# Stick-breaking attention: the sums over keys from a rounded high half and a low half of the summand

## The chip, the core and the metric

The kernel runs on one core of a Trainium2 chip. The metric is the device time of one execution in microseconds (us). Before the change it is 1397.66 us, the median of three runs (1396.64 to 1399.08). The engines are TensorE (PE; its weight loads are listed as PEld), VectorE (DVE), ScalarE (ACT), GpSimd (POOL) and SyncE (SP), which issues the weight transfers.

## What is computed

A decoder trunk of two layers on x of 256 tokens x 1024 features in float32, batch 1: layer 0 is sliding-window attention (16 heads of 64, window 128, sinks) and a dense SwiGLU of 2816; layer 1 is stick-breaking attention (16 heads of 64) and a mixture of 8 experts of 3584 with two chosen for each token; then a final RMSNorm. The change is in the second attention, which the reference gives as:

```
z = einsum(q, k) * scale                                  # query t, key s
log_fail = where(before, log_sigmoid(-z), 0.0)            # before: s < t
between = lax.cumsum(log_fail, axis=3, reverse=True) - log_fail
a = where(before, exp(log_sigmoid(z) + between), 0.0)
out = einsum(a, v) @ w_o
```

The kernel keeps z with keys on the 128 partitions and queries along the free dimension. With softplus(z) = -log_sigmoid(-z), the exponent of a is z minus the sum of softplus over the keys from s up to the query. That is a sum over partitions, so TensorE makes it as a product with a triangular matrix of -1 (and, from the second key block to the first, with a full matrix of -1), added to the z that stands in PSUM.

## The kernel before

Every weight product runs on rounded numbers (the type float32r). A weight unit of 1 MB (128 partitions x 4 x 512) comes by DMA into one of 7 raw slots; ScalarE makes its rounded high half (L528), VectorE its low half, raw minus high (L533), up to three units ahead of TensorE; TensorE adds three products for each pair (high x high, high x low, low x high). A raw slot is loaded again when its low half is done. The inputs of the products (inT_high, inT_low, and hid_high, hid_low in the dense layer and the experts) are split in the same way. All matmuls are recorded on L1354, the transposes on L1406, L1515, L1700 and L1731.

Each engine has its own list of instructions, written out by hand, that it runs in order; semaphores tie the lists together. The eight PSUM banks are given out by a table (`plan`), and the scores of tile b take two banks, (2b) mod 6 and the next.

The second attention goes by feature tiles n = 0 to 7, each with two heads (`half`). For a tile:

- `sb_scores(n)` on TensorE: z = k q in float32 into two banks, 384 columns each: for the first key block 256 queries, for the second the last 128. Then a product of mask_scale with mask_tri (both rounded), which puts -1e30 on what is not before the query. It signals z_ready.
- `clamp(b)` on VectorE (L1164): soft = min(z, 30), 128 x 768, from both banks.
- `log_one_plus_exp(b)` on ScalarE (L851, L853): exponential, then logarithm of 1 + it.
- `soft_plus(b)` on VectorE (L1172): fail = max(z, soft), the summand, float32 in SBUF. It signals fail_ready.
- `sb_sums(n)` on TensorE: three float32 products for each half, with tri or minus_ones as the other operand, onto the z in the banks.
- ScalarE's exponential of the banks (L866) gives stick, the weights a.
- `sb_values(n)` on TensorE: v times stick in float32.

The tiles soft, fail and stick have two buffers each, all in the area `work` (so the profile shows them as work; q is in qT, k and v in kv_area, tri in consts). Scores and clamp of tiles 0 and 1 come before the projection of v, and their maxima during it. Then TensorE runs `sums(n)`, `scores(n+2)`, `values(n-1)` for n = 0 to 8, as far as there are such tiles. VectorE runs, for b = 2 to 7, `clamp(b)`, at b = 5 and 7 the low half of a finished part of the attention's output (L1020), and `soft_plus(b)`. ScalarE runs `stick(c)`, at odd c from 3 on the rounded half of a part of the output (L750), and `log_one_plus_exp(c+2)`. GpSimd has nothing between 57 and 419 us. After the loop comes the output projection wo1, whose first product reads weight units and output parts that are ready by then.

Of the kernel before, what the change touches and what calls it, by code (L numbers as in the profile page):

```python
# [14 lines left out]
P = 128  # L15
# [281 lines left out]
def build(nc, a):  # L297

    ctx = ExitStack()
    with ctx:  # L300
        def sb(name, shape, dt=F32):
            return ctx.enter_context(nc.sbuf_tensor(name, shape, dt))

        def sem(name):
            return ctx.enter_context(nc.semaphore(name))
# [17 lines left out]
        minus_ones = sb("minus_ones", [P, P])  # L323
        bias_tiles = sb("bias_tiles", [QKV_TILES, P])
# [6 lines left out]
        vT_swa = sb("vT_swa", [P, SEQ])  # L331
# [49 lines left out]
        probs = work[:, 2 * w0:3 * w0]  # L381

# [7 lines left out]
        fail = [work[:, (2 + n) * 768:(3 + n) * 768].rearrange("p (a k) -> p a k", a=2) for n in range(2)]  # L390
        stick = [work[:, (4 + n) * 768:(5 + n) * 768].rearrange("p (a k) -> p a k", a=2) for n in range(2)]
# [61 lines left out]
        fail_ready = sem("fail_ready")  # L453
        stick_used = sem("stick_used")
# [188 lines left out]
        def _(pool):  # L643
# [12 lines left out]
            for n in range(2):  # L656
                for m in range(2):
# [14 lines left out]
                                    router_gain[:, :].unsqueeze(2).to_broadcast([P, DT, E]), ALU.mult).then_inc(router_ready, 1)  # L672

# [272 lines left out]
        def _(dve):  # L946
# [5 lines left out]
            def split_to(n):  # L952

                while lows[0] <= n:
                    make_low(dve, lows[0])
                    lows[0] += 1
# [163 lines left out]
            V.tensor_copy(mask_tri[:, :], tri).then_inc(masks_ready, 1)  # L1120
            split_to(AT["wo0"] + SPLIT)
# [39 lines left out]
            def clamp(b):  # L1161
                lo = 2 * b % 6
                dve.wait_ge(z_ready, b + 1)
                V.tensor_scalar(soft[b % 2], bank[:, lo:lo + 2, 0:3 * P], SOFT_TOP, None, ALU.min).then_inc(clamped_ready, 1)  # L1164

            def soft_plus(b):
                lo = 2 * b % 6
                dve.wait_ge(soft_ready, b + 1)
                if b >= 2:
                    for half in range(2):  # L1170
                        full(dve, ("z", b - 2, half))
                V.tensor_tensor(fail[b % 2], bank[:, lo:lo + 2, 0:3 * P], soft[b % 2], ALU.max).then_inc(fail_ready, 1)  # L1172

            clamp(0)
# [3 lines left out]
            soft_plus(1)  # L1178
            for vh in range(2):
                split_to(AT["v1"] + vh + 1 + SPLIT)  # L1180
                for tb in range(TB):
                    b = full(dve, ("v1", vh, tb))
                    freed(V.tensor_copy(v_sb[:, tb, vh * HALF:(vh + 1) * HALF], b), ("v1", vh, tb))
            for b in range(2, FT):
                clamp(b)
                if b >= 5 and b % 2 == 1:
                    input_part_low("oT1", b // 2 - 2)
                soft_plus(b)
            input_part_low("oT1", FT // 2 - 2)
# [162 lines left out]
        def _(pe):  # L1352
# [254 lines left out]
            def sb_sums(n):  # L1607

                pe.wait_ge(fail_ready, n + 1)
                for half in range(2):  # L1610
                    b = bank[:, USES[("z", n, half)][0], :]
                    f = fail[n % 2][:, half, :]
                    mm(b[:, 0:SEQ], tri, f[:, 0:SEQ], False, False, skip_group_check=True)
                    mm(b[:, P:SEQ], minus_ones[:, :], f[:, SEQ:SEQ + P], False, False, skip_group_check=True)
                    ins = mm(b[:, SEQ:SEQ + P], tri, f[:, SEQ:SEQ + P], False, True, skip_group_check=True)
                    filled(ins, ("z", n, half))
# [21 lines left out]
            pe.wait_ge(masks_ready, 2)  # L1638
# [184 lines left out]
```

## Time and profile before

| | |
|---|---|
| median of three runs | 1397.66 us (1396.64 to 1399.08) |
| the profiled execution | 1399.92 us, of which the span is 1398.1 us |
| TensorE, matmul | 1379.1 us busy, 7165 instructions |
| VectorE | 1091.6 us busy |
| ScalarE | 922.9 us busy |
| GpSimd | 43.3 us busy |
| projections of q, k, v of the second attention | to 363 us |
| loop over the eight tiles | 363 to 392.7 us |
| output projection, norm, routing | 392.7 to 430 us |
| experts | 430 to 1380 us |

Times are counted from the start of the span. In a timeline row the first number is the start, the second the length; "x2" are instructions of one kind that follow each other with nothing else between, taken together; the length then reaches from the first start to the last end. Matmuls are pipelined, so their recorded lengths overlap; how long one keeps TensorE is read from start to start. In brackets stands the idle time of the engine before the row, and what ended it.

### The profile page before, as it was taken

Reading aid. Unit: us, or ns where it says so; the run is one execution under the profiler, and the core shown is the slowest. Engines: PE = TensorE matmul, PEld = TensorE weight load, DVE = VectorE, ACT = ScalarE, POOL = GpSimd, SP = SyncE. Lnnn points to the kernel's source line nnn. Section 1 sums busy time; section 2 is a strip of 40 time slices with the busy share of each in tenths; the row PEclk is TensorE's granted clock in tenths of the full one; section 3 lists DMA queues with packets and bytes.
Section 4 is the critical chain, followed back from the end, with each engine's and each line's share of the span. In section 5 each row is a group of like instructions: output and inputs, shape, how many; then the busy total and the mean of one; then the engine's idle time right before and its main releaser. Section 6 shows DMA issues by size and latency. Waiting matters only on the chain.

```text
span 1398.1 us, 19292 instructions
## 1 busy us (share of the span) xinstructions
PE 1379.1 (99%) x7165; PEld 1160.8 (83%) x7165; DVE 1091.6 (78%) x824; ACT 922.9 (66%) x762; POOL 43.3 (3%) x38
## 2 busy tenths in 40 slices
PE   9999999999999999999999999999999999999997
PEld 6879999889887888888888888888888888888885
DVE  5964444464548888988988898888888888889886
ACT  5754333445456777777777777777777777778775
POOL 2100000000000000000100000010000000000000
PEclk9999999999999999999999999999999999999999
DMA  9446553744327999999999999999999999999993
GB/s 324 156 162 206 190 181 122 247 159 158 114 91 292 385 368 358 389 387 371 369 394 374 353 395 389 359 376 394 380 349 394 386 361 373 390 372 359 392 372 124
DMA packets 185102, 430.48 MB, mean 308 GB/s; under 512 B 7047, under 2 KB 12241, under 8 KB 185058
## 3 DMA queue, kind: packets, MB, share of 16 engines
q1 hardware_dynamic: 181344, 417.36, 81.8%
q0 software_dynamic: 2896, 10.03, 2.6%
q10 hardware_dynamic: 818, 2.47, 0.6%
q8 instruction: 31, 0.51, 0.1%
q14 instruction: 13, 0.11, 0.0%
HBM read 422.48 MB, written 7.36 MB: 307 GB/s over the span
## 4 chain that ended last, share of the span: by engine, by line
PE 90%; DVE 5%; DMA 2%; issue 1%; ACT 1%; DVEq 0%; ACTq 0%; POOLq 0%
PE bank L1354 87%; DVE low L533 2%; DMA sum_dram<-qT,slot_row 2%; PE bank L1731 2%; DVE h L984 1%; PE bank L1700 0%; PE bank L1406 0%; PE bank L1515 0%; DMA qT<-in_onehot 0%; DVE work L1275 0%; DVE inT_low L1020 0%; DVE peak L1077 0%; DVE h L1067 0%; DVE work L1067 0%; DVE slot_spare L1281 0%
## 5 line engine op out<-in xcount | busy, mean ns | idle before, releaser
L533 DVE TENSOR_TENSOR low<-raw,high 128x2048 fp32r<-128x2048 f32 (+1 forms) x397 | 898.8, 2276 | 216.4 <-ACT high L528 214.2
L528 ACT CAST high<-raw 128x2048 fp32r<-128x2048 f32 (+1 forms) x397 | 754.8, 1903 | 298.5 <-PE bank L1354 295.2
L1354 PE MATMUL bank<-high,inT_high 128*128 128x512 f32 x1000 | 394.8, 395 | 4.4 <-DVE low L533 2.8
L1354 PE MATMUL bank<-high,inT_low 128*128 128x512 f32 x1000 | 389.9, 390 | 0.0
L1354 PE MATMUL bank<-low,inT_high 128*128 128x512 f32 x1000 | 389.5, 390 | 0.0
L1354 PEld LDWEIGHTS bank<-high,inT_high 128*128 128x128 f32 x1000 | 187.8, 188 | 45.7 <-DVE low L533 5.9
L1354 PEld LDWEIGHTS bank<-high,inT_low 128*128 128x128 f32 x1000 | 187.7, 188 | 39.9
L1354 PEld LDWEIGHTS bank<-low,inT_high 128*128 128x128 f32 x1000 | 187.9, 188 | 37.5
L1354 PE MATMUL bank<-high,hid_high 128*128 128x512 f32 x528 | 207.2, 392 | 0.0
L1354 PE MATMUL bank<-high,hid_low 128*128 128x512 f32 x528 | 205.7, 390 | 0.0
L1354 PE MATMUL bank<-low,hid_high 128*128 128x512 f32 x528 | 205.5, 389 | 0.0
L1354 PE MATMUL bank<-inT_high,high 128*128 128x256 f32 x560 | 159.9, 285 | 0.3 <-DVE inT_low L1020 0.3
L1354 PE MATMUL bank<-inT_low,high 128*128 128x256 f32 x560 | 158.5, 283 | 0.0
L1354 PE MATMUL bank<-inT_high,low 128*128 128x256 f32 x560 | 158.5, 283 | 0.0
L1354 PEld LDWEIGHTS bank<-high,hid_low 128*128 128x128 f32 x528 | 99.1, 188 | 21.0
L1354 PEld LDWEIGHTS bank<-low,hid_high 128*128 128x128 f32 x528 | 99.2, 188 | 20.0
L1354 PEld LDWEIGHTS bank<-high,hid_high 128*128 128x128 f32 x528 | 99.2, 188 | 19.9
L1354 PEld LDWEIGHTS bank<-inT_high,high 128*128 128x128 f32 x560 | 107.7, 192 | 2.2 <-issue 1.9
L1354 PEld LDWEIGHTS bank<-inT_low,high 128*128 128x128 f32 x560 | 107.5, 192 | 0.8 <-issue 0.7
L1354 PEld LDWEIGHTS bank<-inT_high,low 128*128 128x128 f32 x560 | 107.5, 192 | 0.0
L915 ACT ACTIVATE work<-bank 128x512 f32<-128x512 f32 x56 | 33.5, 599 | 45.9 <-PE bank L1354 45.9
L1254 DVE TENSOR_TENSOR hid_low<-bank,hid_high 128x512 fp32r<-128x512 f32 x56 | 38.2, 683 | 0.0
(180 smaller groups left out, 644.2 us busy)
## 6 DMA issues: line engine op xcount, KB each, us to landing
raw<-in_moe_w_gate SPq DMA_DIRECT2D x112, 1024.0 KB, 7.0
raw<-in_moe_w_up SPq DMA_DIRECT2D x112, 1024.0 KB, 7.2
raw<-in_moe_w_down SPq DMA_DIRECT2D x112, 1024.0 KB, 6.9
raw<-in_sb_w_qkv SPq DMA_DIRECT2D x12, 1024.0 KB, 5.3
raw<-in_ffn_w_down SPq DMA_DIRECT2D x11, 1024.0 KB, 4.9
raw<-in_ffn_w_gate SPq DMA_DIRECT2D x10, 1024.0 KB, 5.7
raw<-in_ffn_w_up SPq DMA_DIRECT2D x10, 1024.0 KB, 5.1
raw<-in_swa_w_qkv SPq DMA_DIRECT2D x4, 1024.0 KB, 12.1
```

Of the source, the lines that this page charges most:

```text
L528: nc.scalar.copy(high[n % SPLIT][:, :, 0:c], raw[r][:, :, 0:c]).then_inc(high_done, 1)
L533: nc.vector.tensor_tensor(low[n % SPLIT][:, :, 0:c], raw[n % RAW][:, :, 0:c], high[n % SPLIT][:, :, 0:c].bitcast(F32), ALU.subtract).then_ ...
L915: freed(nc.scalar.activation(e_silu[b % 2], p[0:CAP, :], ACT.Silu), ("g", b))
L984: V.scalar_tensor_tensor(h[:, tb, cols], x[:, tb, cols], rstd[:, tb:tb + 1], gain, ALU.mult, ALU.mult).then_inc(h_ready, 1)
L1254: freed(V.tensor_tensor(hid_low[:, half_of(b)], bank[:, USES[("hidT", b)][0], :], hid_high[:, half_of(b)].bitcast(F32), ALU.subtract), ("h ...
L1354: return nc.tensor.matmul(out, lhsT, rhs, start=start, stop=stop, **kw)
L1731: ins = nc.tensor.transpose(out[:, s * CAP:(s + 1) * CAP], e_prod[b % 2][:, s * P:(s + 1) * P], ident[0:CAP, 0:CAP])
```

## The change

The summand is no longer multiplied in float32. GpSimd makes its rounded high half with a copy into a float32r tile (`fail_high`), as soon as fail is ready and, from tile 2 on, both halves of the sums of tile n-2 are done; VectorE makes the low half, fail minus fail_high (`fail_low`), in a new step `fails_low(b)`. The sums are four rounded products for each half: high and low with minus_round (a rounded copy of minus_ones) for 128 columns, then high and low with mask_tri (the rounded copy of tri) for all 384 columns at once. `sb_sums(n)` waits for both new semaphores. In VectorE's order `fails_low(0)` and `fails_low(1)` come behind the maxima of these tiles, and then `fails_low(b-1)` behind `clamp(b)` and ahead of `soft_plus(b)`, the last one behind `soft_plus(7)`.

The high and low tiles of even tiles lie in hid_high and hid_low, those of odd tiles in two new ones. To make room, vT_swa of the first attention moves into the area h, behind the scores of its first group.

```diff
+        minus_round = sb("minus_round", [P, P], F32R)
+        second_high = sb("second_high", [P, 6 * P], F32R)
+        second_low = sb("second_low", [P, 6 * P], F32R)
...
-        vT_swa = sb("vT_swa", [P, SEQ])
...
+        vT_swa = h[:, :, :].rearrange("p t d -> p (t d)")[:, w0:w0 + SEQ]
...
+        fail_high = [v.rearrange("p (a k) -> p a k", a=2) for v in (hid_high[:, 0:6 * P], second_high[:, :])]
+        fail_low = [v.rearrange("p (a k) -> p a k", a=2) for v in (hid_low[:, 0:6 * P], second_low[:, :])]
...
@@ gpsimd @@
+            for n in range(FT):
+                pool.wait_ge(fail_ready, n + 1)
+                if n >= 2:
+                    for half in range(2):
+                        full(pool, ("z", n - 2, half))
+                nc.gpsimd.tensor_copy(fail_high[n % 2], fail[n % 2]).then_inc(fail_high_ready, 1)
...
@@ vector @@
+            dve.wait_ge(ones_set, 2)
+            V.tensor_copy(minus_round[:, :], minus_ones[:, :]).then_inc(masks_ready, 1)
...
+            def fails_low(b):
+                dve.wait_ge(fail_high_ready, b + 1)
+                V.tensor_tensor(fail_low[b % 2], fail[b % 2], fail_high[b % 2].bitcast(F32),
+                                ALU.subtract).then_inc(fail_low_ready, 1)
...
             soft_plus(0)
             soft_plus(1)
+            fails_low(0)
+            fails_low(1)
...
             for b in range(2, FT):
                 clamp(b)
+                if b >= 3:
+                    fails_low(b - 1)
                 if b >= 5 and b % 2 == 1:
                     input_part_low("oT1", b // 2 - 2)
                 soft_plus(b)
+            fails_low(FT - 1)
...
@@ tensor, sb_sums(n) @@
-                pe.wait_ge(fail_ready, n + 1)
+                pe.wait_ge(fail_high_ready, n + 1)
+                pe.wait_ge(fail_low_ready, n + 1)
                 for half in range(2):
                     b = bank[:, USES[("z", n, half)][0], :]
-                    f = fail[n % 2][:, half, :]
-                    mm(b[:, 0:SEQ], tri, f[:, 0:SEQ], False, False, skip_group_check=True)
-                    mm(b[:, P:SEQ], minus_ones[:, :], f[:, SEQ:SEQ + P], False, False, skip_group_check=True)
-                    ins = mm(b[:, SEQ:SEQ + P], tri, f[:, SEQ:SEQ + P], False, True, skip_group_check=True)
+                    for f in (fail_high[n % 2][:, half, :], fail_low[n % 2][:, half, :]):
+                        mm(b[:, P:SEQ], minus_round[:, :], f[:, SEQ:SEQ + P], False, False, skip_group_check=True)
+                    for f in (fail_high[n % 2][:, half, :], fail_low[n % 2][:, half, :]):
+                        ins = mm(b[:, 0:SEQ + P], mask_tri[:, :], f, False, f is not None, skip_group_check=True)
                     filled(ins, ("z", n, half))
...
-            pe.wait_ge(masks_ready, 2)
+            pe.wait_ge(masks_ready, 3)
```

## Rows read from the trace of the kernel before

**Rows 1.** The page: busy time of the engines, and the chain by engine.
```profile
PE 1379.1 (99%) x7165; PEld 1160.8 (83%) x7165; DVE 1091.6 (78%) x824; ACT 922.9 (66%) x762; POOL 43.3 (3%) x38
...
PE 90%; DVE 5%; DMA 2%; issue 1%; ACT 1%; DVEq 0%; ACTq 0%; POOLq 0%
```

**Rows 2.** Busy time by stretch, the loop and the experts; columns in the first line.
```profile
core 0: us, PE busy (x) PEld busy (x) DVE busy (x) ACT busy (x) POOL busy (x), PEclk, DMA share, GB/s
363.00:392.70 29.70, 29.46 (x222) 23.53 (x220) 13.65 (x16) 18.08 (x31) 0.00 (x0) 1.00 0.11 36
...
430.00:1380.00 950.00, 947.02 (x4314) 782.72 (x4315) 843.02 (x544) 706.50 (x474) 26.80 (x14) 1.00 1.01 372
```

**Rows 3.** Timeline of TensorE, one pass of the loop (sums(3) to sums(4)).
```profile
374.00 0.70 PE L1354 MATMUL bank<-work,consts 128*128 128x256 f32 x2
374.54 0.38 PE L1354 MATMUL bank<-work,minus_ones 128*128 128x128 f32 x2
374.76 0.82 PE L1354 MATMUL bank<-work,consts 128*128 128x128 f32 x4
...
375.96 0.92 PE L1354 MATMUL bank<-qT,kv_area 64*128 64x256 f32 x8
376.81 0.50 PE L1354 MATMUL bank<-mask_tri,mask_scale 128*128 128x256 f32 x2
...
378.04 0.70 PE L1354 MATMUL bank<-work,consts 128*128 128x256 f32 x2
```

**Rows 4.** Timeline of TensorE: sums(2), sums(7) and the start of wo1.
```profile
369.97 0.70 PE L1354 MATMUL bank<-work,consts 128*128 128x256 f32 x2
...
389.19 0.70 PE L1354 MATMUL bank<-work,consts 128*128 128x256 f32 x2 [0.24 <-DVE work L1172]
...
392.68 0.50 PE L1354 MATMUL bank<-high,inT_high 128*128 128x512 f32 x1
```

**Rows 5.** Timeline of VectorE: clamps of tiles 2, 4, 5 and maxima of 2, 3.
```profile
366.21 0.96 DVE L1164 TENSOR_SCALAR work<-bank 128x768 f32<-128x768 f32 x1 [2.35 <-PE bank L1354]
368.95 0.96 DVE L1172 TENSOR_TENSOR work<-bank,work 128x768 f32<-128x768 f32 x1 [1.78 <-ACT work L853]
...
372.56 0.96 DVE L1172 TENSOR_TENSOR work<-bank,work 128x768 f32<-128x768 f32 x1 [1.78 <-ACT work L853]
373.43 0.95 DVE L1164 TENSOR_SCALAR work<-bank 128x768 f32<-128x768 f32 x1
...
377.35 0.96 DVE L1164 TENSOR_SCALAR work<-bank 128x768 f32<-128x768 f32 x1 [0.22 <-PE bank L1354]
```

**Rows 6.** Timeline of TensorE: rounded products of 256 and of 512 columns.
```profile
292.79 0.28 PE L1354 MATMUL bank<-inT_high,low 128*128 128x256 f32 x1
292.90 0.28 PE L1354 MATMUL bank<-inT_high,high 128*128 128x256 f32 x1
...
354.81 0.39 PE L1354 MATMUL bank<-high,inT_high 128*128 128x512 f32 x1
355.04 0.39 PE L1354 MATMUL bank<-low,inT_high 128*128 128x512 f32 x1
```

**Rows 7.** Timeline of GpSimd, whole span.
```profile
31.57 1.09 POOL L660 TENSOR_SCALAR_AFFINE_SELECT kv_area<-work 128x1024 f32<-128x1024 f32 x1 [21.97 <-PE bank L1354]
...
34.72 3.14 POOL L663 TENSOR_SCALAR_AFFINE_SELECT kv_area<-work 128x1024 f32<-128x1024 f32 x1
53.99 2.90 POOL L552 TENSOR_TENSOR work<-work,inverse 128x1024 f32<-128x1024 f32 x2 [16.13 <-DVE inverse L1090]
```

**Rows 8.** Timeline of VectorE: weight splits, and its idle times that cover edits.
```profile
33.85 3.06 DVE L533 TENSOR_TENSOR low<-raw,high 128x2048 fp32r<-128x2048 f32 x1 [5.01 <-ACT high L528]
...
78.81 0.69 DVE L1020 TENSOR_TENSOR inT_low<-bank,inT_high 128x512 fp32r<-128x512 f32 x1 [2.37 <-ACT inT_high L750]
...
354.28 2.29 DVE L533 TENSOR_TENSOR low<-raw,high 128x2048 fp32r<-128x2048 f32 x1 [3.14 <-ACT high L528]
```

**Rows 9.** Busy time by stretch before and in the clock's fall (columns as in Rows 2).
```profile
285.40:289.00 3.60, 1.31 (x8) 0.84 (x8) 2.95 (x7) 1.24 (x4) 0.00 (x0) 1.00 0.00 0
289.00:292.40 3.40, 3.24 (x11) 2.44 (x11) 2.66 (x6) 2.51 (x5) 0.00 (x0) 0.51 0.05 8
```

More of the change, by code:

```diff
@@ L453, in build @@
         fail_ready = sem("fail_ready")
+        fail_high_ready = sem("fail_high_ready")
+        fail_low_ready = sem("fail_low_ready")
         stick_used = sem("stick_used")
```

## The prediction

> **What bounds the kernel now.** I read the page's busy shares and chain first: TensorE is busy 99% of the span and carries 90% of the chain that ended last [rows 1]. Then the busy time by stretch [rows 2]: in the second attention's loop (363.0 to 392.7 us) TensorE is busy 29.46 of 29.70 us, GpSimd does nothing and the DMA engines are used to 0.11; in the expert stage behind it TensorE is busy 947 of 950 us. So TensorE's own work sets the end in both, and time gained or lost in the loop should reach the end unchanged: nothing later is seen that waits for data by more than 3 us in all.
>
> Then the loop, in the order of time. It makes eight passes (feature tile n = 0 to 7), each of sums(n), scores(n+2), values(n-1). One pass lasts 378.04 - 374.00 = 4.04 us: sums 1.96 (to 375.96), scores 0.85 (to 376.81), mask and values the rest [rows 3]. Scores of n+2 are complete at 376.81 + 0.50 = 377.31, which is 3.31 after sums(n) began. VectorE's clamp starts 0.04 later [rows 3, 5]. From a clamp (366.21) to its maximum (368.95) is 2.74, in which ScalarE does its exponential and logarithm; the maximum takes 0.96, and the sums start 0.06 after its end (369.91 to 369.97) [rows 4, 5]. That chain, 0.04 + 2.74 + 0.96 + 0.06 = 3.80, lies beside a whole pass and more of TensorE's work, so TensorE waits only before sums(7), 0.24 us [rows 4].
>
> **The change part by part.**
>
> *Sums.* Today a half has one float32 matmul of 256 columns and two of 128. Each is recorded as two instructions: the pair of 256 takes 0.43 us (0.54 from 374.00, with about 0.1 of the first weight load), the pair of 128 takes 0.22 [rows 3]. Two halves are 2 x (0.43 + 0.22 + 0.22) = 1.74; the other 0.22 of 1.96 is load and turnover at the ends, and stays. The new half has two rounded matmuls of 128 columns and two of 384. Rounded operands take one instruction, 0.12 us for 256 columns and 0.23 for 512 [rows 6]; 384 lies between, 0.17. No row has a rounded one with 128 moving columns. Bounds: 0.11 (hardly less than the 0.12 of 256 columns, where the load of 128 weight columns has to fit too), and 0.22, what the float32 pair takes. So the sums take 4 x 0.17 + 4 x (0.11 to 0.22) + 0.22 = 1.34 to 1.78, a saving of 0.62 to 0.18. Both rows are one step away from it, so I take the middle, 0.40 saved. If TensorE still set the pace, that would be 8 x 0.40 = 3.2 us gained.
>
> *GpSimd's rounding.* 128 x 768, one input, in SBUF. GpSimd's selects of 128 x 1024 took 1.09 us, times 768/1024 = 0.82; its two-input products took 2.90 for 1536 columns, so 1.45; one select took 3.14, so 2.36 [rows 7]. No row excludes that a rounding copy is slower, and none gives less than 0.82. I take 0.82, the one-input row. With 0.05 for each handover it is 0.92 in the chain. Nothing else is queued on GpSimd until 419 us.
> The 3.14 us select ran while VectorE had a subtraction of two SBUF operands, which took 3.06 instead of 2.29 [rows 7, 8]: both were held up. The Trainium skill (SBUF — State Buffer, "SBUF: two separate sides") has the rule: the port pair that the two share is an exclusive lock, held for a whole instruction, and a VectorE operation with two SBUF inputs contends with a GpSimd operation that reads SBUF. By that rule these rows agree, and by it the lock bites in this change only before the loop (rounding of tile 1 beside the subtraction of tile 0), since later each subtraction waits for its own rounding.
> The Trainium skill (GPSIMD Engine Reference, "When to use GPSIMD") says that one-input work is roughly at line rate there and two-input work about twice slower than on VectorE; the rows above carry the price without it.
>
> *VectorE's low half.* A subtraction with two SBUF inputs: 2.29 us for 2048 columns, 0.96 for 768 columns of a maximum or clamp [rows 5, 8]; I take 0.96. It is issued behind the NEXT clamp: clamp(b), low(b-1), maximum(b). So low(b-1) waits not for its rounding alone but for scores(b), which TensorE does only after sums(b-2). This is the wait that matters: TensorE's sums(b-1) stand behind it, and scores(b+1) behind these.
>
> *The ring that forms.* From sums(b-2) to scores(b) complete: 3.31 - 0.40 = 2.91; to the clamp 0.04; clamp 0.87 (373.43 is 0.87 after 372.56, so two operations in a row overlap a little); low 0.96; to sums(b-1) 0.06. One turn is 2.91 + 0.04 + 0.87 + 0.96 + 0.06 = 4.84 us per pass (4.62 to 5.06), against 4.04 today and 3.64 of TensorE work. The maximum and the rounding have to fit in the same turn: the maximum ends 2.74 + 0.96 = 3.70 after its clamp, the rounding 0.92 later is 4.62, and low starts at 4.84 + 0.87 = 5.71; GpSimd is hidden in the middle passes up to 3.70 + 0.10 + x = 5.71, x = 1.91 us.
>
> *The sum.* Clamp(2) comes 0.40 earlier, 365.81; its maximum runs 368.55 to 369.51; clamp(3) 369.42 to 370.38; rounding 369.56 to 370.38; low(2) 370.43 to 371.39; sums(2) 371.45, where they were at 369.97 [rows 4, 5]. Sums(5) are three turns on, 385.97. Clamp(7) starts 2.95 later, 388.92; then, with no further clamp in the way, 3.70 + 0.05 + 0.82 + 0.05 + 0.96 + 0.06 = 5.64 gives sums(7) at 394.56 (389.19 today). From there to the next projection were 3.49 (392.68), now 3.09: 397.65, which is 4.97 later. Bounds: the saving in the sums counts six times in this path (once before clamp(2), three turns, once up to clamp(7), once at the end), so 3.65 at 0.62 saved and 6.29 at 0.18. Each microsecond more of rounding counts twice (before sums(2), before sums(7)): 1.26 more at 1.45.
>
> *At nothing.* The cast of the minus ones, 128 x 128, some 0.2 us at 74 us: VectorE idles 2.37 us at 78.81 [rows 8]; without that cover it would cost its 0.2. Low(0) and low(1) with their roundings, at most 4 x 0.96 = 3.8 us, stand ahead of the weight split before the one at 354.28; ahead of that one VectorE idles 3.14 us [rows 8], and the splits run up to three weight units ahead of TensorE, so I see nobody late. Raw slots come free some 3 us later in a stretch where the DMA engines have time. Without the cover the loop would start up to 1 us late. The move of the transposed values into h adds no instruction and no wait.
>
> The profiled execution is 1398.1 us of span in 1399.92; the sum makes it 1403.1 in 1404.9. That run is 2.3 above the median, so on the median: 1397.66 + 5.0 = 1402.7.
>
> **The rivals.**
> 1. TensorE stays the bound (the other side): the loop becomes 8 x 0.40 = 3.2 us shorter (1.4 to 5.0), 1394.5. For it: today TensorE waits for nearly nothing, and VectorE is busy 13.65 of 29.7 us. It decides only if what lies between scores(b) and sums(b-1) beside the 2.91 is under 3.64 - 2.91 = 0.73; the rows make it 0.04 + 0.87 + 0.96 + 0.06 = 1.93. Against it, therefore, the order on VectorE.
> 2. The sums shrink by more than my upper end. Each 0.1 more per pass takes 0.6 off the loss; at 0.77 saved the loss is 2.8 and drops into what can't be told from no change: about 1399.5.
> 3. GpSimd's copy is slow, as in the 3.14 row (2.36): two passes take at least 2.95 + 3.70 + 0.10 + 2.36 + 0.96 + 0.06 = 10.13, 5.07 each, and the two ends 1.54 more each: 5.0 + 3.1 + some 0.5 = 8.6, 1406.3.
> 4. The clock falls. It is at 0.51 from 289.0 to 292.4, after 3.6 us in which TensorE was busy 1.31 [rows 9]. In my schedule it idles 2.3 us before sums(2) (values(0) would end at 369.97 - 0.80 = 369.17), 1.2 in each middle pass, 1.4 before sums(7). One such fall of 3.4 us at half the clock costs up to 1.7 us, since sums and scores are in the ring: 5.0 + 1.3, 1404.0. Against it: the loop is busy three quarters of the time.
> 5. The sums are no cheaper at all (both rounded sizes at the float32 step): excluded for 384 by the rows of 256 and 512; for 128 it is my upper bound.
>
> **How the numbers follow.** The ring as worked out (3.6 to 6.3, 1401.3 to 1404.0) 0.50; GpSimd slow 0.13; clock 0.09; the smaller loss 0.16; TensorE bound 0.12. A measurement of this kernel tells about 0.2% (2.8 us) from no change. So slower 0.72, same 0.16, faster 0.12. The likeliest case gives 1402.7. The range leaves out the faster case, a third of the smaller loss and the top of the slow copy: 1398.5 to 1407.
>
> **What would show it.** In the timeline of the changed kernel: sums of 1.3 to 1.8 us; passes of 4.6 to 5.1 us in the middle; TensorE idle about 1.2 us before each sums, released by VectorE's low half, and 2.3 before sums(2); VectorE's low half starting right behind the clamp of the next tile, not at the end of its rounding; GpSimd's copy near 0.8; the next projection near 397.7; the expert stage as long as before. The prediction is wrong if low halves start before the next scores are there, if passes last 3.6 us, if the copy takes over 1.9, or if the expert stage gives the loss back.

## The result, and the profile after

The changed kernel takes 1403.84 us (median of six runs, 1402.56 to 1404.72) beside 1399.02 for the kernel before on the same chip; the ratio, computed from all executions and not from the two medians, is 1.0037, with a 95% interval of 1.0024 to 1.0050. That is 4.8 us slower by the medians, and the direction is clear of the noise; the size is less so. The kernel before took 1399.02 us over its six runs here, of which the first three alone gave 1397.66, and 1397.6 to 1397.8 in the four larger groups of runs below. Beside those the changed kernel is 6.0 to 6.3 us slower. The profiled execution has a span of 1400.4 us.

The page's busy times and chain after, the lines that answer to [rows 1]:

```profile
PE 1372.8 (98%) x7133; PEld 1154.0 (82%) x7133; DVE 1099.2 (78%) x833; ACT 923.6 (66%) x762; POOL 50.7 (4%) x46
...
PE 91%; DVE 5%; issue 2%; ACT 1%; DMA 0%; DVEq 0%; POOL 0%; ACTq 0%; POOLq 0%
```

TensorE is busy 6.3 us less over the span, 4.7 of them in the loop (24.76 us below, 29.46 in [rows 2]), and the kernel is slower: the work was saved, the time was not. Where it went is read from the same stretches as in [rows 2], with the loop where it now lies:

```profile
360.50:394.20 33.70, 24.76 (x189) 18.47 (x187) 19.10 (x22) 19.18 (x31) 4.96 (x6) 1.00 0.10 32
422.20:425.60 3.40, 3.40 (x6) 1.56 (x6) 2.66 (x15) 2.12 (x2) 0.00 (x0) 0.50 0.64 254
430.00:1380.00 950.00, 946.95 (x4326) 783.23 (x4325) 841.91 (x547) 705.73 (x473) 26.81 (x14) 1.00 1.01 373
```

The loop was 29.71 us with TensorE busy in all but 0.24; it is 33.71 us (360.50 to 394.21) with TensorE idle for 8.9. The experts are as they were. One pass of it on TensorE, the timeline that answers to [rows 3] and [rows 4] (start, length, then instruction; in brackets the idle time ahead of it):

```profile
368.87 0.30 PE L1380 MATMUL bank<-hid_high,minus_round 128*128 128x128 f32 x1 [2.54 <-DVE hid_low L1192]
...
378.23 0.30 PE L1380 MATMUL bank<-hid_high,minus_round 128*128 128x128 f32 x1 [1.21 <-DVE hid_low L1192]
378.36 0.27 PE L1380 MATMUL bank<-hid_low,minus_round 128*128 128x128 f32 x1
378.48 0.39 PE L1380 MATMUL bank<-hid_high,mask_tri 128*128 128x384 f32 x1
378.71 0.34 PE L1380 MATMUL bank<-hid_low,mask_tri 128*128 128x384 f32 x1
378.88 0.22 PE L1380 MATMUL bank<-hid_high,minus_round 128*128 128x128 f32 x1
378.94 0.27 PE L1380 MATMUL bank<-hid_low,minus_round 128*128 128x128 f32 x1
379.05 0.39 PE L1380 MATMUL bank<-hid_high,mask_tri 128*128 128x384 f32 x1
...
379.55 0.92 PE L1380 MATMUL bank<-qT,kv_area 64*128 64x256 f32 x8
380.40 0.50 PE L1380 MATMUL bank<-mask_tri,mask_scale 128*128 128x256 f32 x2
380.83 0.87 PE L1380 MATMUL bank<-work,kv_area 128*64 128x256 f32 x8
382.91 0.30 PE L1380 MATMUL bank<-second_high,minus_round 128*128 128x128 f32 x1 [1.21 <-DVE second_low L1192]
...
391.35 0.30 PE L1380 MATMUL bank<-second_high,minus_round 128*128 128x128 f32 x1 [1.58 <-DVE second_low L1192]
...
394.21 0.50 PE L1380 MATMUL bank<-high,inT_high 128*128 128x512 f32 x1
```

The sums take 1.32 us (378.23 to 379.55) where they took 1.96, the pass takes 4.68 (378.23 to 382.91) where it took 4.04, and 1.21 of it TensorE waits for VectorE's low half. VectorE and GpSimd in the same pass, the timeline that answers to [rows 5] and [rows 7]:

```profile
379.00 0.96 DVE L1188 TENSOR_TENSOR work<-bank,work 128x768 f32<-128x768 f32 x1 [0.32 <-ACT work L867]
380.94 0.96 DVE L1180 TENSOR_SCALAR work<-bank 128x768 f32<-128x768 f32 x1 [0.98 <-PE bank L1380]
381.82 0.95 DVE L1192 TENSOR_TENSOR second_low<-work,second_high 128x768 fp32r<-128x768 f32 x1
```

```profile
346.27 1.65 POOL L686 CAST second_high<-work 128x768 fp32r<-128x768 f32 x1
...
380.03 0.83 POOL L686 CAST second_high<-work 128x768 fp32r<-128x768 f32 x1 [3.85 <-DVE work L1188]
```

The rounding of tile 5 ends at 380.86. Its low half could start then; it starts at 381.82, right behind the clamp of tile 6, and that clamp waited 0.98 us for TensorE's scores. This is the ring of the prediction, a circle of waits in which each step stands behind the one before it, from one sums to the next: 2.67 (378.23 to the end of the mask's products, 380.90) + 0.04 + 0.88 + 0.95 + 0.14 = 4.68.

**Stages.** Each traced execution here is cut at four starts: sums(0), the first product of wo1, the first product of the experts, the end of the span. For the kernel before they are 362.97, 392.68, 430.18 and 1398.1; for the changed one 360.50, 394.21, 432.62 and 1400.4. The last two columns say how long the clock was at half in the loop and behind it, in the routing.

| kernel | sums(0) starts | loop | wo1 and routing | experts to end | half clock in loop | in routing |
|---|---|---|---|---|---|---|
| before | 362.97 | 29.71 | 37.5 | 967.9 | 0 | 0 |
| changed | 360.50 | 33.71 | 38.4 | 967.8 | 0 | 3.4 |
| changed, again | 358.52 | 35.82 | 37.5 | 967.7 | 6.8 | 0 |

So the loop costs 4.00 us more. The span of the changed execution is only 2.3 us longer because it came to the loop 2.47 us earlier, while a fall of the clock at 422.2 adds 0.9 to the routing: -2.47 + 4.00 + 0.92 - 0.1 = 2.3. The 2.47 have two parts. TensorE's first transposes in the norm ahead of the projections, in the kernel before and in the changed one:

```profile
287.12 1.32 PE L1406 MATMUL bank<-consts,h 128*128 128x128 f32 x8 [1.72 <-DVE h L984]
```

```profile
286.02 1.32 PE L1432 MATMUL bank<-consts,h 128*128 128x128 f32 x8 [1.72 <-DVE h L998]
```

From there to sums(0) it is 75.85 us before and 74.48 after. These 1.37 us are the clock, which fell at 289.0 in the one [rows 9] and stayed at 1.00 there in the other. The other 1.10 were there before the norm, and they are not the change either: in the second trace of the changed kernel the same transposes start at 284.04, and from them to sums(0) it is again 74.48.

### The profile page after: what moved, and what is told of

It is laid out like the page before. It is cut to its first block, busy times and chain, and to the rows that moved or that the text cites. A ratio compares the mean times of both kernels' runs of the same rounds, so it can differ in the third digit from the quotient of the medians.

```text
span 1400.4 us, 19259 instructions
## 1 busy us (share of the span) xinstructions
PE 1372.8 (98%) x7133; PEld 1154.0 (82%) x7133; DVE 1099.2 (78%) x833; ACT 923.6 (66%) x762; POOL 50.7 (4%) x46
## 3 DMA queue, kind: packets, MB, share of 16 engines
q10 hardware_dynamic: 818, 2.47, 0.5%
## 4 chain that ended last, share of the span: by engine, by line
PE 91%; DVE 5%; issue 2%; ACT 1%; DMA 0%; DVEq 0%; POOL 0%; ACTq 0%; POOLq 0%
PE bank L1380 89%; DVE low L540 2%; PE bank L1758 2%; DVE h L998 0%; PE bank L1727 0%; DVE work L1301 0%; PE bank L1541 0%; DMA qT<-in_onehot 0%; DVE inT_low L1034 0%; PE bank L1432 0%; DVE second_low L1192 0%; DVE peak L1091 0%; ACT inT_high L764 0%; DVE h L1081 0%; DVE hid_low L1192 0%
```

## The experiments

There is one profile for each kernel. Times are medians, with the ratio to the kernel before on the same chip (1397.8, 1397.8, 1397.8 and 1397.6 us in the four groups of runs). In the code cuts "..." stands for lines left out.

**Low half ahead of the clamp.**

```diff
             for b in range(2, FT):
-                clamp(b)
                 if b >= 3:
                     fails_low(b - 1)
+                clamp(b)
```

> VectorE's low half of tile b-1 is issued ahead of the clamp of tile b instead of behind it; nothing else differs from the changed kernel, whose loop (sums(0) to the first product of wo1) lasts 33.71 us. Theory (a ring through VectorE's list): low, clamp (0.88 later), maximum (2.74 later), 0.96, rounding 0.83 and two handovers of 0.05 now follow each other in every pass: 5.5 us from sums to sums against 4.68, five passes, loop 37.8 to 38.7 us, the kernel 4 to 5 us slower than the changed one. Rival (the sums only wait for their own rounding, VectorE's order is nothing): the low half starts at the end of its rounding, the loop is 33.7 or up to 4 us shorter.

Measured: 1411.97 us, ratio 1.0089 (1.0053 to 1.0125), loop 41.02. The first full pass, at a full clock, on VectorE:

```profile
368.19 0.96 DVE L1192 TENSOR_TENSOR hid_low<-work,hid_high 128x768 fp32r<-128x768 f32 x1 [0.93 <-POOL hid_high L686]
369.06 0.95 DVE L1180 TENSOR_SCALAR work<-bank 128x768 f32<-128x768 f32 x1
371.80 0.96 DVE L1188 TENSOR_TENSOR work<-bank,work 128x768 f32<-128x768 f32 x1 [1.79 <-ACT work L867]
373.68 0.96 DVE L1192 TENSOR_TENSOR second_low<-work,second_high 128x768 fp32r<-128x768 f32 x1 [0.93 <-POOL second_high L686]
```

The low half now waits 0.93 us for its rounding, as the rival wants, and yet the pass is 5.50 us (sums at 369.29 and 374.79), as the ring through VectorE's list says: everything follows in a row. Of the two places tried, behind the clamp is the better. The loop is 2.3 us above the upper end of what I expected, and the clock accounts for it. It falls from 374.8 to 385.0, after TensorE idled 2.02 us, and again for 10.2 us from 391.9 on, after 1.57. The first fall costs nothing, since the five passes from sums(2) (369.29) to sums(7) (396.78) still take 27.49 us, five times 5.50; under the second the end of the loop, from sums(7) to wo1, takes 5.16 us instead of 2.86.

```profile
371.00:374.80 3.80, 1.78 (x19) 1.14 (x15) 2.07 (x3) 1.53 (x3) 0.83 (x1) 1.00 0.00 0
374.80:385.00 10.20, 10.20 (x43) 7.59 (x43) 5.37 (x7) 5.48 (x9) 1.66 (x2) 0.50 0.01 2
```

**No low half.** `fails_low` and its wait are left out, and both products of each kind read fail_high, so the result is no longer that of the reference; TensorE has as many products of the same sizes.

```diff
-                pe.wait_ge(fail_low_ready, n + 1)
...
-                    for f in (fail_high[n % 2][:, half, :], fail_low[n % 2][:, half, :]):
+                    for f in (fail_high[n % 2][:, half, :], fail_high[n % 2][:, half, :]):
```

> Leaves out the low half: no subtraction on VectorE, and TensorE multiplies the rounded half twice in its place, so its instructions are as many and as long as in the changed kernel. Theory (ring): without low, sums(b) wait for clamp-to-maximum and rounding only, two passes take 2.67 + 0.04 + 3.70 + 0.05 + 0.83 + 0.1 = 7.4 us, 3.7 each; loop 28.5 us (28 to 29.5), 5.2 less than the changed kernel and about 1 less than before (29.71). Rival (GpSimd is what holds TensorE): the loop keeps most of its 33.7, at least 32.5.

Measured: loop 28.56, 1397.02 us, ratio 0.9996 (0.9985 to 1.0007). Two passes take 7.39 us (368.77 to 376.16), and in the middle TensorE hardly waits:

```profile
376.16 0.44 PE L1375 MATMUL bank<-hid_high,minus_round 128*128 128x128 f32 x2 [0.28 <-POOL hid_high L686]
```

Without the low half 5.15 us of the loop go: 1.09 ahead of sums(2), 3.94 in the four middle passes, and the rest behind them. So the rounding alone does not hold TensorE at 4.68. But 3.94 / 4 is 0.98 for each middle pass, about the length of the low half, so this run alone doesn't tell its length from its place in the list; the run above, which moves it, and the scores earlier, below, do. GpSimd's rounding, still there, is waited for 0.28 us at most in the middle, and 1.46 and 1.40 us before sums(2) and sums(7). The time is 0.8 us below that of before, which the interval does not tell from nothing.

**Rounding twice.**

```diff
...
+                nc.gpsimd.tensor_copy(spare, fail[n % 2]).then_inc(spare_done, 1)
+                pool.wait_ge(spare_done, n + 1)
                 nc.gpsimd.tensor_copy(fail_high[n % 2], fail[n % 2]).then_inc(fail_high_ready, 1)
```

> GpSimd makes a second copy of 128 x 768 into a spare area ahead of each rounding, some 0.88 us more. Theory: GpSimd is hidden in the middle passes (its rounding ends 0.96 before the low half starts) and counts at the two ends only: middle passes stay at 4.68 to 4.75, the loop is 2 x 0.88 = 1.8 longer, 35.5 us. Rival (GpSimd in the ring): each of six passes longer by 0.88, loop 39 us.

Measured: 1409.37 us (two runs), ratio 1.0082 (1.0053 to 1.0111), loop 39.09. By the total the rival would win; the passes say otherwise. TensorE at each wait:

```profile
370.31 0.45 PE L1384 MATMUL bank<-hid_high,minus_round 128*128 128x128 f32 x1 [3.44 <-DVE hid_low L1196]
377.10 0.30 PE L1384 MATMUL bank<-second_high,minus_round 128*128 128x128 f32 x1 [0.85 <-DVE second_low L1196]
381.77 0.30 PE L1384 MATMUL bank<-hid_high,minus_round 128*128 128x128 f32 x1 [1.21 <-DVE hid_low L1196]
386.45 0.30 PE L1384 MATMUL bank<-second_high,minus_round 128*128 128x128 f32 x1 [1.21 <-DVE second_low L1196]
391.12 0.30 PE L1384 MATMUL bank<-hid_high,minus_round 128*128 128x128 f32 x1 [1.21 <-DVE hid_low L1196]
395.79 0.30 PE L1384 MATMUL bank<-second_high,minus_round 128*128 128x128 f32 x1 [2.48 <-DVE second_low L1196]
```

The middle passes stay at 4.68, and each of the two ends is 0.90 longer (the wait before sums(2) 3.44 instead of 2.54, before sums(7) 2.48 instead of 1.58): 1.8 us, as expected. The other 3.6 us are the clock. It falls in the longer idle time, from 368.9 to 375.7, which makes the pass from sums(2) to sums(3) 6.79 instead of 4.68 (2.1), and again for 3.4 us from 396.3, where the end of the loop takes 4.35 instead of 2.86 (1.5).

```profile
368.90:375.70 6.80, 5.39 (x22) 4.17 (x24) 2.40 (x3) 2.05 (x4) 1.93 (x3) 0.50 0.00 0
```

**Float32 sums behind the same waits.** `sb_sums` keeps both waits and has the three float32 products of the kernel before.

> The sums are again three float32 products for each half, but still wait for high and low as in the changed kernel. It prices the shorter sums inside the ring. Theory: sums take 1.96 instead of 1.32, and this counts in every turn, six times: middle passes 5.32, loop 33.7 + 3.8 = 37.5 us, the kernel some 4 us slower than the changed one. Rival (the sums lie beside VectorE's work and their length is hidden): passes stay at 4.68, loop 34 to 35 us.

Measured: passes 5.29, loop 37.35, 1406.63 us, ratio 1.0064 (1.0041 to 1.0087). TensorE idles the same 1.21 us in each pass, though it works longer:

```profile
375.26 0.67 PE L1380 MATMUL bank<-work,consts 128*128 128x256 f32 x2 [1.21 <-DVE second_low L1192]
380.55 0.67 PE L1380 MATMUL bank<-work,consts 128*128 128x256 f32 x2 [1.21 <-DVE hid_low L1192]
```

So the shorter sums are in the ring and do bring their 3.6 us (37.35 - 33.71); the waits for the two halves cost 7.6 (37.35 - 29.71), and the change nets the two.

**The changed kernel again.**

> The changed kernel once more, for its loop and for where the clock falls. Theory: the loop is 33.7 us again and the middle passes 4.68; what the time is above before by more than 4.0 us comes from the clock: a fall in the loop (TensorE idles 2.5 us before sums(2)) or after it, which differs from one execution to the next. Rival: the loop's length itself varies, or the experts' stage is longer by itself at a full clock.

Measured: 1404.00 us (1401.79 to 1412.60), ratio 1.0060 (1.0038 to 1.0081). The profiled loop is 35.82: all passes are those of the first profile except the one from sums(2) to sums(3), 6.78, where the clock was at half from 366.3 to 373.1. It fell in the 2.54 us of idle time before sums(2):

```profile
362.70:366.30 3.60, 1.65 (x16) 0.99 (x14) 2.34 (x3) 2.44 (x5) 0.83 (x1) 1.00 0.00 0
366.30:373.10 6.80, 6.21 (x26) 4.45 (x26) 2.79 (x4) 2.53 (x5) 0.83 (x1) 0.50 0.00 0
```

**Scores one tile earlier**, in the changed kernel and, as a control, in the kernel before:

```diff
             for n in range(FT + 1):
-                if n < FT:
-                    sb_sums(n)
                 if n + 2 < FT:
                     sb_scores(n + 2)
+                if n < FT:
+                    sb_sums(n)
                 if n >= 1:
                     sb_values(n - 1)
```

> The changed kernel with TensorE's order scores(n+2), sums(n), values(n-1) instead of sums(n), scores(n+2), values(n-1). The scores of tile n+2 then wait only for their banks, given free by the exponential of tile n-1, and no longer stand behind the sums that wait for the low half. Theory (the ring closes through sums, scores, clamp, low): it opens, TensorE has 3.40 us of work per pass (1.32 + 0.85 + 0.43 + 0.80) and ScalarE's order allows 3.35 to 3.65; loop 26 to 28 us, 2 to 3.5 us faster than before and 6 to 7.5 faster than the changed kernel. Rival (VectorE's total chain is simply too long): passes stay above 4.2, the loop above 31 us.

> The kernel before with the same new order of TensorE. Control: there TensorE was full (29.46 of 29.70 us), so the order has nothing to give: loop 29.7 us (29.4 to 30.5), the time that of before within 0.1%. If it got faster too, the gain of the run beside it would be the order's alone and not the rounded sums'.

Measured, changed kernel with the new order: 27.39 us from sums(0) to wo1, middle passes 3.61, 1398.51 us, ratio 1.0008 (1.0000 to 1.0017). The work is the same and the pass is 1.07 shorter: the ring is open, since the scores no longer stand behind the sums. TensorE's longest waits are now at the end, where no scores are left, and 0.67 before scores(3), for banks.

```profile
359.36 0.92 PE L1380 MATMUL bank<-qT,kv_area 64*128 64x256 f32 x8
...
360.55 0.22 PE L1380 MATMUL bank<-hid_high,minus_round 128*128 128x128 f32 x1
...
362.53 0.92 PE L1380 MATMUL bank<-qT,kv_area 64*128 64x256 f32 x8 [0.67 <-ACT work L880]
...
377.86 0.30 PE L1380 MATMUL bank<-second_high,minus_round 128*128 128x128 f32 x1
...
381.46 0.30 PE L1380 MATMUL bank<-hid_high,minus_round 128*128 128x128 f32 x1 [1.43 <-DVE hid_low L1192]
```

These loops can't be compared as they stand. In the new order scores(2) stand ahead of sums(0), from 359.36 to 360.55, so a loop counted from sums(0) leaves 1.19 us of its work out. Counted from the first product behind the v projection it is 28.58 us, which is 5.13 less than the changed kernel's 33.71 and 1.13 less than the 29.71 of before (in the old order sums(0) come right behind the projection, and both ways of counting agree).

Measured, kernel before with the new order: 28.25 us from sums(0), 29.44 from the first product behind the v projection, passes 3.85, 1397.53 us, ratio 1.0001 (0.9993 to 1.0010). The loop is 0.27 shorter and the time 0.3, which is the control that was expected. In a middle pass the order by itself saves 0.19, by turnovers: sums behind the mask's product take 1.85 us (as sums(1) do in the kernel before) and behind the values' 1.96, and the product behind the mask's starts 0.34 later and not 0.43. Most of that goes again, 0.67 us of it in waiting before scores(3). So of the 5.13 us the order's own share is 0.27, and the rest is the opened ring.

In the new order the rounded sums are worth 0.86 us of loop (29.44 - 28.58), although a middle sums takes 1.31 us instead of 1.85. TensorE's own work would allow passes of 1.31 + 0.80 + 0.85 + 0.34 = 3.30; they take 3.61. The rows name the ring that is left, on VectorE and then on ScalarE:

```profile
367.64 0.96 DVE L1188 TENSOR_TENSOR work<-bank,work 128x768 f32<-128x768 f32 x1 [0.76 <-ACT work L867]
368.51 0.95 DVE L1180 TENSOR_SCALAR work<-bank 128x768 f32<-128x768 f32 x1
...
371.25 0.96 DVE L1188 TENSOR_TENSOR work<-bank,work 128x768 f32<-128x768 f32 x1 [0.77 <-ACT work L867]
```

```profile
369.50 0.84 ACT L865 ACTIVATE work<-work 128x768 f32<-128x768 f32 x1 [0.56 <-DVE work L1180]
370.37 0.85 ACT L867 ACTIVATE work<-work 128x768 f32<-128x768 f32 x1
```

Maximum, clamp of the next tile right behind it, exponential, logarithm, next maximum: 0.87 + 0.99 + 0.87 + 0.88 = 3.61. The clamp could start earlier, since the mask's product of its scores ended at 367.12, 1.39 us before it; it stands behind the maximum in VectorE's list. A clamp ahead of the maximum was not run, so that this order would give more is not shown.

**Scores and logarithm earlier.** As the run above, with `log_one_plus_exp(c + 2)` moved to the top of ScalarE's loop.

> As scores_earlier, and ScalarE does the exponential and logarithm of tile c+2 ahead of the exponential of tile c. Theory: with the scores early, ScalarE's order is what is left of the ring (logarithm behind the exponential of the sums); with it turned the loop comes to TensorE's own 25 to 26.5 us, 3 to 4.5 us less than before. Rival: the banks come free later, since the exponential that frees them now waits behind the logarithm, and the loop is no shorter than that of scores_earlier.

Measured: 39.78 us from sums(0), 1410.14 us, ratio 1.0086 (1.0068 to 1.0104): the rival, and far beyond it. The exponential that frees the banks now waits, behind the logarithm, for a clamp that waits for scores, and the next scores wait for these banks. Passes take 5.0 to 6.0, and the clock falls three times in the loop on top. The ring of 3.61 was not ScalarE's order to open: in the rows above ScalarE waits 0.56 us for the clamp.

**Fillers.** Float32 products without a result, 0.22 us each, in TensorE's idle time: ahead of the wait in sums(2) to sums(7) of the changed kernel, and in sums(6) and sums(7) of the kernel with earlier scores.

```diff
+            def beside(n, count):
...
+                for half in range(2):
+                    taken(pe, ("z", n - 1, half))
+                b = bank[:, USES[("z", n - 1, 1)][0], :]
+                for _ in range(count):
+                    mm(b[:, 0:P], tri, tri, True, True)
...
             def sb_sums(n):
...
+                beside(n, {2: 9, 3: 5, 4: 5, 5: 5, 6: 5, 7: 6}.get(n, 0))
                 pe.wait_ge(fail_high_ready, n + 1)
```

> The changed kernel with TensorE kept at work in its idle time: behind values(n-1) and ahead of the wait for the halves stand 9 float32 products of 128 columns (0.22 us each) for sums(2), 5 for sums(3) to sums(6), 6 for sums(7), into a bank that nobody reads. They add no result and fit into the idle time of 2.5, 1.2 and 1.6 us. Theory (the ring costs 4.0 us, and what the changed kernel loses beyond that is the clock falling in its idle loop, 0 us in one traced execution and 2.1 in the other): the clock stays up in the loop, the loop is 33.7 to 34.0 us, the kernel 1401.5 to 1402.3 where before is 1397.8, about 1.5 to 2 faster than the changed one, with no execution above 1405. Rival (the rest comes from elsewhere): the time stays at 1403.8 to 1404 with the same spread, or grows by the fillers that overrun.

> scores_earlier with the same fillers, 5 each ahead of sums(6) and sums(7), where its TensorE idles 1.43 us each. Its times lie in two groups, about 1397 and 1399.7, and its one traced execution, the fastest, had no fall of the clock from 11.6 us on. Theory (the slower group has a fall in or near the loop's end): the loop is 27.4 to 27.6 us and the median falls from 1398.5 to 1396.5 to 1397. Rival (the falls are elsewhere, in the norms and the routing, which every kernel here has): the median stays at 1398 to 1399.

> scores_earlier once more, to see in a second traced execution where the clock falls. Theory: the loop is 27.4 us whenever the clock holds, and a slower execution shows a fall of 3.4 us or more, each worth about 1 to 2.5 us. Rival: the loop's length itself varies by 2 to 3 us at a full clock.

Measured, changed kernel filled: the loop is 33.72, as expected, the slowest of five executions 1405.75 (1412.60 of six without fillers), but the median is 1403.56, ratio 1.0039 (1.0027 to 1.0052), not 1401.5 to 1402.3. In its trace the clock holds in the loop, as it did in one of the two without fillers. The interval overlaps that of the kernel without fillers (1.0038 to 1.0081), so what the fillers bring is not resolved, and the 1.5 to 2 us that I expected are not shown. The profile shows the clock falling outside: 3.4 us at 289.4 and 3.4 us at 426.0 (routing 38.4).

Measured, earlier scores filled: 1397.09 us, ratio 0.9998 (0.9990 to 1.0007), 27.37 us from sums(0); earlier scores again: 1396.93 us, ratio 0.9995 (0.9986 to 1.0004), 27.38. The two don't differ, so the fillers have nothing to do there. The same kernel took 1398.51 us in the group before, with the same loop: 1.6 us between two groups of runs is more than most of the differences looked for here. Both profiles have the clock at half in the norm (289.4; 287.2) and for 6.8 us in the routing, which then takes 40.1 us:

```profile
413.30:416.90 3.60, 3.60 (x30) 3.12 (x28) 2.06 (x5) 3.28 (x5) 0.87 (x2) 1.00 0.02 5
416.90:423.70 6.80, 6.80 (x17) 3.70 (x16) 3.65 (x16) 3.45 (x4) 0.99 (x3) 0.50 0.40 154
```

Ahead of the fall TensorE had the transposes of x and the router's products, 8 columns each. In this execution the fall costs 2.6 us, more than the 1.1 by which the loop is shorter than before; but it is one of the slower ones (1399.61 us), and what the median execution loses there no trace shows.

**More fillers in the norm ahead of the projections.** In the kernel with earlier scores, `keep_clock(("hT2", 3), 2)` becomes 4.

> scores_earlier with two more float32 products of 512 columns (0.86 us each, no result) in TensorE's wait of 1.72 us in the norm ahead of the second attention's projections. In most traced executions the clock falls there for 3.4 us (before: at 289.0), and the loop then starts 2.4 us later (363 against 360.5 us). Theory: the fall is due to that idle time, the loop starts at 360.5 in every execution, the loop stays 27.4 us; median 1395 to 1396, 2 to 3 us less than before, if the routing behind the loop keeps its 37.1 to 39.7 us. Rival: the clock falls there all the same (the transposes and the second, shorter wait are enough), or falls later instead, and the median stays at 1397 to 1398.

Measured: 1397.02 us, ratio 0.9998 (0.9989 to 1.0007). The profiled execution has no fall in the norm, sums(0) at 360.68, 27.38 us from there to wo1, a fall of 3.4 us in the routing (38.4), and a span of 1394.2; the median is nevertheless that of the run without them. A fall in the norm was never worth the 2.4 us of the expectation but 1.4 (see the stages above), and the first trace with the scores earlier, without these fillers, has no fall there either. I can't tell from one profile where the other executions lose time.

In the next table "loop" is counted from sums(0), and in the column behind it from the first product behind the v projection.

| kernel | sums(0) starts | loop | from v projection | wo1 and routing | half clock in loop | in routing |
|---|---|---|---|---|---|---|
| low half first | 360.92 | 41.02 | 41.02 | 40.1 | 20.3 | 6.8 |
| no low half | 361.49 | 28.56 | 28.56 | 40.1 | 0 | 6.8 |
| rounding twice | 361.05 | 39.09 | 39.09 | 40.2 | 10.2 | 6.8 |
| float32 sums | 361.00 | 37.35 | 37.35 | 38.5 | 0 | 3.4 |
| changed, filled | 363.33 | 33.72 | 33.72 | 38.4 | 0 | 3.4 |
| scores earlier | 360.55 | 27.39 | 28.58 | 37.5 | 0 | 0 |
| scores earlier, again | 362.30 | 27.38 | 28.57 | 40.1 | 0 | 6.8 |
| scores earlier, filled | 364.50 | 27.37 | 28.57 | 40.1 | 0 | 6.8 |
| scores earlier, norm filled | 360.68 | 27.38 | 28.58 | 38.4 | 0 | 3.4 |
| before, scores earlier | 362.94 | 28.25 | 29.44 | 37.5 | 0 | 0 |
| scores and logarithm earlier | 362.68 | 39.78 | 40.97 | 39.0 | 16.1 | 4.4 |

**What of this reaches the time.** The time of an execution is longer than its span: by 1.75 to 1.89 us in every one of these runs of the kernel before and of before with the new order, and by 2.16 us or more in every run of the changed kernel and its variants but rounding twice (1.87). So some 0.4 us of the loss lie outside the span; what makes them is not shown. With the loop from the first product behind the v projection, each less that of before:

| kernel | loop | loop and 0.4 | median |
|---|---|---|---|
| changed | +4.0 | +4.4 | +4.8 |
| changed, again | +4.0, +6.1 in its trace | +4.4 to +6.5 | +6.2 |
| changed, filled | +4.0 | +4.4 | +5.8 |
| no low half | -1.15 | -0.75 | -0.8 |
| scores earlier | -1.1 | -0.7 | +0.7 |
| scores earlier, again | -1.1 | -0.7 | -0.8 |
| scores earlier, filled | -1.1 | -0.7 | -0.7 |
| scores earlier, norm filled | -1.1 | -0.7 | -0.5 |
| before, scores earlier | -0.3 | -0.3 (without the 0.4) | -0.3 |

In the lower six rows loop and 0.4 give the median to within 0.2 us but for one, so nothing more has to be explained there; in that one and in the upper rows up to 1.8 us stay open.

## Why the prediction was right, point by point

- **What bounds the kernel: right.** TensorE's list, full in the loop and with the experts; the loss in the loop went through to the end, the experts' stage is 967.7 to 967.9 us in all three traces of the first table and 967.4 to 968.2 in all fourteen.
- **Sums: mis-sized.** I took 1.56 from bounds of 1.34 and 1.78 and measured 1.32, below the lower one. The rounded product of 128 columns was the unknown: the second of a pair starts 0.06 us after the first (378.88, 378.94) and the next product 0.11 after that, 0.17 a pair where my lower bound was 0.22. Those of 384 columns take 0.23 and 0.17, 0.20 on average, where I had 0.17. I should have seen that the 0.11 of the weight load can lie beside a longer product before it (the load for the product of 378.88 starts at 378.71, together with the product ahead of it); the middle between the bounds had no reason but that both rows were equally far.
- **GpSimd's rounding: right.** 0.83 us, I took 0.82, the one-input row. Hidden in the middle and counted at both ends: shown by rounding twice. The idle times of TensorE are 2.54, 1.21 and 1.58 us where I had 2.3, 1.2 and 1.4.
- **The low half: right.** 0.95, I took 0.96.
- **The ring: right in its place and parts**, shown by runs from different sides: without the low half the pass is 3.70, with the low half moved it grows to 5.50, and with scores earlier it opens (3.61) while all the work stays. The last two keep the low half's length and change only what it stands behind or what stands behind it, so they show that its place counts. Its turn is 4.68 in 4.62 to 5.06. Another term was mis-sized: from the end of the low half (382.77) to the sums (382.91) it is 0.14, where I used the 0.06 of a float32 product behind the maximum.
- **The sum.** With 0.64 saved in the sums instead of 0.40 my path gives 4.97 - 6 x 0.24 = 3.53; with 0.08 more at each of five handovers, 3.93. The loop measured 4.00. So the forecast of 5.0 for the loop was 1 us too high, inside its own bounds (3.65 to 6.29).
- **That 4.8 and 5.0 lie so close is luck.** The loop gives 4.0, and some 0.4 lie outside the span, which the sum had not at all. What is left is 0.4 us beside the kernel before of these six runs and 1.8 beside that of the larger groups, where the loss is 6.2 and my 5.0 is too small. A part can be the clock rival, to which I gave 0.09: in one of two traces of the changed kernel the clock fell in the idle time before sums(2), and it cost 2.1 us there, above my 1.7 at most, as it stayed down for 6.8 us and not for 3.4. How often it does so is not shown, and the filled kernel, whose one traced loop held the clock, is still 5.8 us slower than before: the share of the clock stays open.
- **The rivals.** TensorE as the bound: refuted for the change; even with the scores earlier the pass is 3.61 and not TensorE's 3.30. GpSimd slow: refuted. At nothing, both right: low(1) ended at 348.91, the delayed split at 351.11, and the loop began without a wait; the cast of the minus ones is covered, VectorE idling 2.21 us behind it instead of 2.37.
- The Trainium skill (SBUF — State Buffer, "SBUF: two separate sides") holds that a VectorE operation with two SBUF inputs and a GpSimd operation that reads SBUF lock each other out for a whole instruction. The one place where a rounding and a subtraction meet in the changed kernel agrees: the rounding of tile 1, issued beside the subtraction of tile 0 (346.27, both), took 1.65 us instead of 0.83, and the subtraction its usual 0.96.

## What to carry to other kernels

When a faster operation needs one more step from another engine, price the step by its place in that engine's list, not by its length: a rounding of 0.83 us and a subtraction of 0.95, on two engines that were idle half the time or more, cost 7.6 us of loop, most of it because the subtraction's place closed a ring between TensorE and VectorE, and the shorter products gave back only 3.6. Before such a change look for what stands behind the new wait: here it was TensorE's next scores, and with these issued first the same change has a loop of 28.6 us instead of 33.7. Compare passes, not totals: a total of 39.1 us matched the wrong theory, because a fall of the clock was in it. And when an edit moves work across the mark from which a stage is counted, move the mark: counted from sums(0), the new order seemed to save 6.3 us where it saves 5.1, and 1.5 in the control where it saves 0.3.

No version here beats the kernel before by more than its interval. The changed kernel with earlier scores is 5.5 us faster than the changed one on the same chip (1398.51 and 1404.00) and the same as before within 0.2%: its loop is 1.1 us shorter, and 0.4 of that go again outside the span.

## What the hardware showed that I had not expected

- TensorE's clock went to 0.50 of full speed, so to 1.2 from 2.4 GHz, in stretches of 3.4, 6.8 or 10.2 us. All fourteen traces also show it at half in their last 5 us, and some in the first 16. In the loop it fell in or right behind idle times of TensorE of 2.54 and 3.44 us, and also after 2.02 and 1.57 (low half first). The same 2.54 us were passed at a clock of 1.00 in the first trace of the changed kernel, and its middle passes, with 1.21 us idle in each, ran at 1.00 in both. In the norm TensorE was busy 1.31 of 3.6 us ahead of the fall [rows 9], and in the routing it was at transposes and products of 8 columns.
- The same kernel loses the clock in different places in different executions: the changed one at 422.2 in one and at 366.3 in the other. One such stretch costs 1.4 us in the norm ahead of the loop (75.85 against 74.48 from its transposes to sums(0)), 0.9 or 2.6 in the routing (3.4 or 6.8 us long), 2.1 in the ring (6.8 us long), and nothing in the passes of 5.50 where TensorE waits for others anyway. For this kernel that is of the size of what was looked for.
- A rounded product of 128 columns can follow another in 0.06 us (378.88, 378.94), about half of the 0.11 of a float32 instruction of that size, of which a float32 product needs two.
